# Low halves of the weight slots in two attention stretches: computed by POOL, in step order between its loads, instead of by DVE

## The reference

```
for layer in range(DEPTH):
    xn = rms_norm(h, norm_g[layer])
    mem_kv = mem_n @ mem_w_kv[layer]
    mixed = even_layer(...) if layer % 2 == 0 else odd_layer(...)   # concat of three gated branches, 2560 wide
    h = h + (mixed @ w_out[layer]).astype(h.dtype)
return rms_norm(h, final_norm_g)

# one attention head and block of 128 queries
s = einsum('bqhd,bkhd->bhqk', qi, k) * scale + bias;  s = where(causal, s, NEG_INF)
p = softmax(s);  o = einsum('bhqk,bkhd->bqhd', p, v);  y = o * silu(gate)
```

## Time and profile before

| | |
|---|---|
| three timed runs | 2295.04, 2295.32, 2296.09 us (median 2295.32) |
| profiled execution, first to last instruction (its span) | 2293.4 us |
| around the span, against the median | 1.9 us |
| PE busy | 2255.4 us, 98% |
| DVE busy | 998.4 us, 44% |
| ACT busy | 823.4 us, 36% |
| POOL busy | 402.1 us, 18% |
| granted TensorE clock, mean | 0.998 |
| chain that ended last, PE's share | 96% |

### The profile page before, as it was taken

How to read it: one execution, slowest core, us unless ns; L and a number is a source line. 1 busy time by engine, 2 the same in 40 slices (tenths; PEclk the granted TensorE clock), 3 DMA queues, 4 the chain that set the end, 5 groups by cost and what they waited for, 6 DMA issues and landing times.

```text
span 2293.4 us, 30844 instructions
## 1 busy us (share of the span) xinstructions
PE 2255.4 (98%) x11901; PEld 1831.9 (80%) x11901; DVE 998.4 (44%) x1865; ACT 823.4 (36%) x1457; POOL 402.1 (18%) x691
## 2 busy tenths in 40 slices
PE   7999999999999999999999999999999999999998
PEld 7888887787788878888788778888887866788886
DVE  4632455444522256643353442442122356666534
ACT  6533333333332434432342223322232444555323
POOL 1626113222221011100010001100000254221100
PEclk9999999999999999999999999999999999999999
DMA  7645444434445346563344446444443665454632
GB/s 281 205 136 138 132 112 126 125 115 136 117 116 189 102 159 197 176 222 101 117 145 122 133 144 226 129 133 151 153 123 97 210 201 168 144 194 135 227 102 92
DMA packets 166923, 345.65 MB, mean 151 GB/s; under 512 B 21535, under 2 KB 32111, under 8 KB 164355
## 3 DMA queue, kind: packets, MB, share of 16 engines
q1 hardware_dynamic: 106832, 188.51, 27.3%
q0 software_dynamic: 31248, 98.44, 13.5%
q10 hardware_dynamic: 28707, 56.84, 6.8%
HBM read 279.89 MB, written 63.83 MB: 150 GB/s over the span
## 4 chain that ended last, share of the span: by engine, by line
PE 96%; issue 1%; DVE 1%; ACT 1%; DMA 1%; DVEq 0%; POOL 0%; SPq 0%; ACTq 0%; POOLq 0%
PE PS L241 79%; PE PS L1699 3%; PE PS L2365 2%; PE PS L1688 2%; PE PS L291 1%; PE PS L1122 1%; PE PS L2262 1%; PE PS L558 1%; PE PS L1870 1%; PE PS L2225 1%; PE PS L1448 1%; PE PS L2014 1%; PE PS L2258 1%; PE PS L1895 1%; PE PS L1118 1%
## 5 line engine op out<-in xcount | busy, mean ns | idle before, releaser
L241 PE MATMUL PS<-A,wsp 128*128 128x512 f32 (+2 forms) x5184 | 1160.4, 384 | 1.7 <-ACT stage L344 1.2
L241 PEld LDWEIGHTS PS<-A,wsp 128*128 128x128 f32 (+1 forms) x5184 | 942.3, 188 | 198.6 <-issue 8.8
L210 DVE TENSOR_TENSOR wsp<-wraw,wsp 128x1024 fp32r<-128x1024 f32 (+1 forms) x358 | 432.8, 1210 | 991.7 <-ACT wsp L203 990.6
L241 PE MATMUL PS<-wsp,A 128*128 128x512 f32 x2928 | 752.0, 401 | 3.6 <-DVE stage L1770 1.7
L203 ACT ACTIVATE wsp<-wraw 128x1024 fp32r<-128x1024 f32 (+1 forms) x358 | 372.1, 1042 | 911.2 <-PE PS L241 879.2
L241 PEld LDWEIGHTS PS<-wsp,A 128*128 128x128 f32 x2928 | 532.1, 189 | 103.9 <-issue 9.1
L344 ACT ACTIVATE stage<-PS 128x512 f32<-128x512 f32 (+1 forms) x150 | 87.1, 587 | 141.3 <-PE PS L241 136.7
L1735 ACT ACTIVATE S<-PS 128x256 f32<-128x256 f32 (+3 forms) x160 | 62.9, 393 | 121.9 <-PE PS L1688 121.0
L1743 ACT ACTIVATE S<-PS,stats 128x256 f32<-128x256 f32 (+3 forms) x160 | 74.8, 467 | 74.8 <-DVE stats L1780 63.6
L1699 PEld LDWEIGHTS PS<-S 128*128 128x128 f32 x640 | 93.0, 191 | 10.3 <-issue 1.1
L1699 PE MATMUL PS<-S 128*128 128x128 f32 x640 | 94.3, 274 | 0.6 <-issue 0.6
(11 more groups left out here) (342 smaller groups left out, 1729.4 us busy)
## 6 DMA issues: line engine op xcount, KB each, us to landing
wraw<-in_even_w_in_dram SPq DMA_DIRECT2D x112, 512.0 KB, 3.7
wraw<-in_odd_w_in_dram SPq DMA_DIRECT2D x88, 512.0 KB, 3.6
wraw<-in_w_out_dram SPq DMA_DIRECT2D x80, 512.0 KB, 3.7
wraw<-in_mem_w_kv_dram SPq DMA_DIRECT2D x32, 512.0 KB, 4.5
yO<-stage ACTq DMA_DIRECT2D x12, 1024.0 KB
yE<-stage ACTq DMA_DIRECT2D x10, 1024.0 KB
S<-yO POOLq DMA_DIRECT2D x36, 256.0 KB, 3.5
hA<-stage ACTq DMA_DIRECT2D x8, 1024.0 KB
```

What stands on the lines that cost most here:

```text
L210: nc.vector.tensor_tensor(wsp[:, q, 1, :, 0:j["cols"]], wraw[:, q, :, 0:j["cols"]], wsp[:, q, 0, :, 0:j["cols"]].bitcast(F32), ALU.subtrac ...
L241: mm = nc.tensor.matmul(dst, lhs, rhs, start=(s == 0 and kk == 0 and i == 0), stop=(s == j["spc"] - 1 and kk == 1 and i == 2))
```

## The change

DVE's part of the 34 splits in the two stretches is taken out of `dve_seq`. `pool_seq` is rewritten: the first head's loads and `qk(1)`, `gate(0)` come first, as before; then POOL goes through the steps, at each of which it first computes the low half of a slot where the plan has one, then issues the loads that are due at that step: `v(H)` and `gate(H)` two steps before the values of head H, `qk(H+1)` at the first step of head H. DVE waits, before it splits slot 4 of OUT0B and of OUT1B, until POOL has done slot 3, so that `w_lo` rises in order. The two slots ahead of SEQ0 and the four in the last pair of MLA heads stay with DVE.

```
@@ dve_seq
-                seq_split(dve, lambda e, n, q, r: dve_slot(e, j, n, q), t, t.splits.get(x, ()))
                 if x < len(t.units):
                     seq_max(dve, t, x)
@@ pool_seq
             n = len(t.start)
-            for H in range(n):
-                if H == 0 and early == 0:
-                    qk(0)
-                if H == 0 and n > 1:
-                    v(0)
-                    qk(1)
-                    gate(0)
-                    continue
-                v(H)
-                if H + 1 < n:
-                    qk(H + 1)
-                gate(H)
+            if early == 0:
+                qk(0)
+            v(0)
+            qk(1)
+            gate(0)
+            for x in range(t.steps):
+                seq_split(pool, lambda e, n_, q, r: pool_slot(e, t.fill, n_, q), t, t.splits.get(x, ()))
+                for H in range(1, n):
+                    if x == t.start[H - 1] + LV + 2:
+                        v(H)
+                        gate(H)
+                    if x == t.start[H] and H + 1 < n:
+                        qk(H + 1)
+
+        def pool_slot(pool, j, n, q):
+            pool.wait_ge(w_lo, n)
+            pool.wait_ge(w_hi, n + 1)
+            nc.gpsimd.tensor_tensor(wsp[:, q, 1, :, 0:j["cols"]], wraw[:, q, :, 0:j["cols"]],
+                                    wsp[:, q, 0, :, 0:j["cols"]].bitcast(F32), ALU.subtract).then_inc(w_lo, 1)
@@ the DVE program, for OUT0B and likewise for OUT1B
             for c in range(4):
+                if c == 0:
+                    dve.wait_ge(w_lo, OUT0B["slot0"] + 4)
                 dve_chunk(dve, OUT0B, c, ...)
```

More of the change, by code:

```diff
@@ L2789, in _ @@
             for c in range(4):
+                if c == 0:
+                    dve.wait_ge(w_lo, OUT1B["slot0"] + 4)
                 dve_chunk(dve, OUT1B, c, lambda s: dve_out(dve, OUT1B, c - 1, 32) if c and s == 2 else dve_gain(dve, c - 1) if c and s == 5 else None, 0 if c else 4)
```

## The result

Five executions of the changed kernel took 2303.04 to 2304.93 us (median 2304.25); a sixth, at 5026.89 us, was disturbed and is left out here and in every comparison. Six of the kernel before, on the same chips, took 2295.04 to 2296.90 us (median 2295.26). The ratio is 1.0034, with an interval of 1.0023 to 1.0046: the change makes the kernel 0.34% slower, 7.8 us by the ratio and 9.0 by the medians. The profiled execution took 2304.25 us, with a span of 2302.6 us where the one before had 2293.4, so 9.2 us are to be found in the trace. The prediction was 2297.7 us, with 2293.5 to 2302.5 as its range.

What follows compares the result with a forecast made beforehand. PE was taken as the bound, with 5.9 us of gaps in the two stretches; -2.5 + 2.3 + 1.1 + 0.5 + 1.0 = +2.4 us on 2293.4 gave 2295.8, forecast as a 2297.7 us median, range 2293.5 to 2302.5.

Steps and rivals of the forecast that it cites:

- Waits for the exponential: Three PE waits in front of NSA scores, SEQ1 steps 19, 43 and 79, would go: -2.5 us at best.
- Step 12: SEQ0: POOL's difference gets in before DVE's L1809 and holds it, delaying the first addition; +2.3 us on PE.
- Step 108: SEQ1: POOL's difference holds DVE's L1809, so the maximum comes late; +1.1 us.
- Normalisations: DVE's normalisations held by POOL's differences, mostly hidden, some tenths late in shorter SEQ1 steps; +0.5 us, bounds 0 and 2.
- POOL's difference: Duration taken for each 128x1024 difference on POOL: 2.41 us, bounds 2.12 and 2.63.
- Maxima blocked: Rival: maximum L1780 also stands for POOL, or a difference takes 4 us; +14 us and more, 2312 us; chance 0.07.
- Loads behind the differences: Value loads issued after POOL's differences in SEQ0 and SEQ1 land late for PE; +1.0 us, bounds 0 and 7.
- The wait at 881 us: SEQ0: values of head 1, behind the differences of steps 3 to 6, land late; +0.6 us, up to 2.8.
- step 38: SEQ0: values of head 9, behind that step's difference, land at 978.56 against 978.43; +0.1 us, up to 2.3.
- behind no difference of their own step: All other value loads either come two steps and more ahead of need or follow no difference in their step.
- The clock: In SEQ0 and SEQ1 the clock is 1.00, so nothing is to be won there; no cost counted.
- rival of late loads: Landing near its upper end at three value loads: up to +7 us instead of +1.0, 2300 to 2304; chance 0.18.

Runs made afterwards that it cites:

- e6: Kernel before, with DVE's low half moved behind the maximum and the normalisation of its step; 2290.43 us, ratio 0.9978.
- e4: Changed kernel, but DVE keeps the low halves of steps 12 and 108; 2303.55 us, ratio 1.0036.
- e2: Changed kernel, but SP's weight loads in the two stretches also wait until PE has used slot n-7; 2298.25 us, ratio 1.0012.
- e3: Changed kernel's order of loads, but DVE computes all low halves and POOL only waits for them before its loads; 2299.07 us, ratio 1.0017.
- e8: Kernel before, with the low half L1809 of one finish at step 12 computed four times in a chain; 2299.09 us, ratio 1.0017.
- e1: Changed kernel, but at each step POOL issues the due loads ahead of its low half; 2301.48 us, ratio 1.0028.
- e5: Changed kernel with POOL's loads ahead of the low half and DVE keeping the low halves of steps 12 and 108; 2296.34 us, ratio 1.0004.
- e7: Changed kernel with SP's weight loads also waiting for PE and DVE keeping the low halves of steps 12 and 108; 2293.79 us, ratio 0.9992.

## Why the prediction was wrong, step by step

The direction of the sum was right and its size was not: +2.4 us predicted, +9.2 measured in the span. By its own terms (predicted, measured in matmul rows):

- *Waits for the exponential*: -2.5, -2.5 in that row. The removal was right, its size too small: e6 shows 5.2 to be had, so "all other low halves on DVE were hidden" does not hold. The changed kernel gains 2.5 us in the NSA heads, up to step 95, net of the new waits below.
- *Step 12*: +2.3, +2.0. *Step 108*: +1.1, +0.9. POOL got the lock both times, DVE ended 0.5 us after it. e4 takes both waits away.
- *Normalisations*: +0.5, +1.1, two waits of 0.54 and 0.55 us behind the differences of the NSA steps 43 and 79.
- *POOL's difference*: 2.41 us taken, 2.37 the median. *Maxima blocked*: not so.
- *Loads behind the differences*: +1.0, +6.2. **This is the term that failed.** The prediction named it, with bounds 0 and 7, and took the landing time of the loads from the earlier trace rows, 3.4 us, measured where POOL issued them at moments of its own. Behind the difference they are issued at the instant at which SP is let go, and land in 5.7 (`vE`) and 4.7 us (`vmD`). e2 and e3 show this from both sides. The wait at 881 us came as 1.7 (0.6 predicted), that of step 38 as 2.05 (0.1 predicted), the one of the memory heads of SEQ1, for which 0.3 stood in the sum, as 1.50, and a fourth, which the prediction did not see, as 0.92 us near 999 us in the next memory head of SEQ0. This last one is a misreading of the plan: step 42 has a slot, and the values of head 10 are due in it, just as those of head 9 at step 38, so "behind no difference of their own step" was not true of it. A load of ACT's queue runs beside it too, and its 6.1 us to landing are not SP's alone. The prediction looked past SP's queue at this point: it priced SP's next load as having slack of its own, which is true, and not as traffic for others.
- *The clock*: 0, +1.7 behind the wait at step 38. "The clock is 1.00 in both, so nothing is to be won there" left out that it can be lost there. e8 shows the cost by itself.

The measured terms make -2.5 + 2.0 + 0.9 + 1.1 + 6.2 + 1.7 = +9.4, against 9.2. That they meet so closely is in part luck: two of them are off by about 1 us in opposite ways. Every trace holds the same 11901 matmuls in the same order, so one can read how much later than in the kernel before the same matmul starts. In us, at places given by the time in the kernel before:

| place | 880 | 892 | 905 | 975 | 989.5 | 1007 | 1130 | 1152 | 1500 | 1940 | 2105 | 2134 | 2144 | 2155 |
|---|---|---|---|---|---|---|---|---|---|---|---|---|---|---|
| changed kernel | -0.2 | 1.8 | 3.8 | 3.8 | 7.7 | 8.9 | 8.9 | 8.9 | 8.9 | 9.0 | 6.4 | 6.6 | 8.3 | 9.2 |
| e6_dve_split_last | 0.2 | 0.2 | 0.2 | 0.2 | 0.2 | 0.2 | 0.2 | 0.2 | 0.2 | 0.0 | -4.6 | -5.2 | -5.2 | -5.5 |
| e8_dve_late | 0.0 | 0.0 | 3.8 | 3.8 | 3.8 | 3.8 | 3.8 | 5.0 | 5.0 | 5.7 | 5.7 | 5.7 | 5.6 | 5.7 |

The four late loads with the half clock behind one of them cost 2.0, 3.9, 1.2 and 1.8 us, 8.9 in all where the rows of waits and the clock gave 7.9; step 12 costs 2.0 and step 108 0.9, as in the rows. The NSA heads gain 2.5 us net, where the rows gave 1.4 (2.5 less 1.1). So the term that failed was about 7.2 us instead of 1.0, and the term of the exponential about 4 us instead of 2.5. What happened is the rival of late loads, to which the prediction gave 0.18 and 2300 to 2304 us; that rival counted landing times alone, and ends just below the 2304.25 measured.

What stays open: not every wait of this size brings the lower clock. That of 2.73 us at step 12 of the changed kernel brought none, nor did 2.25 and 2.03 us in e4; e2's 2.73 at the same step 12 did, and so did 2.05 (the changed kernel), 2.13 (e4), 2.88 (e8) and 3.55 us (e1). That is five of eight, and behind shorter waits of PE in the two stretches, up to 1.7 us, there was none. And behind a wait of some 4 us after SEQ0, which ends near 1142 us in the kernel before and which no edit here touches, the clock stayed low for 3.4 us in before, after, e4 and e6, and for 6.8 us in e1, e2, e3, e5, e7 and e8. By the starts of the same matmuls the longer stretch costs 0.7 to 1.2 us in their spans, and another 0.2 to 0.7 us is lost between 1500 and 1940 us; none of the edits explains either, so single terms of these experiments are not to be read more finely than about 1 us.

## What to carry to other kernels

Before work is moved to an engine that also issues loads, look up who else its semaphore releases: a small load directly behind the instruction that lets a large one go lands beside it, and the landing time from the old trace does not hold. Ask first whether the order on the old engine can be changed instead; here the low half only had to stand behind the maximum, and one moved line gave 5.2 us where the move to another engine cost 9. Where PE waits for a chain of other engines, read the waits of its weight loads beside those of its matmuls, and give every new wait of 2 us and more a second price, the stretch at half clock that can follow it (here behind five of eight).

## What the runs showed of the hardware that was not expected

- Two loads from POOL's queue, issued within 0.1 to 0.2 us of a 512 KB load on SP's queue, landed after 5.8 us (`vE` at 877 us) and 5.4 us (`vmD` at 979 us) in the changed kernel; the same two landed after 3.1 and 2.6 us in e2, where SP's load had been issued 2.4 and 3.6 us ahead.
- Behind a wait of PE of 2.05 us (after) and 2.88 us (e8) the granted clock stood at 0.5 for 3.4 us, though it had been at 1.00 and PE nearly all the time busy before. Behind waits of 2.73 us (after) and 2.25 us (e4) it stayed at 1.00.
- One fp32 difference of 128x1024 on POOL takes 2.37 us, 1.9 times DVE's 1.22; a DVE difference of 128x512 that starts beside it takes 2.7 instead of 0.69 us, and 3.6 us in e1, where its recorded start is 0.68 us ahead of POOL's.
